# Second mixer of a two-block transformer kernel: score products in split single-pass form, weight units between near steps, releases by tile, gates by tanh, two weight splits moved

## The reference

```python
x = x + rms_norm(hybrid_mixer(rms_norm(x, g1), ...), g2)
x = x + rms_norm(conv_ffn(rms_norm(x, g3), ...), g4)
```

```python
proj = hn @ w_in          # a_qk, a_v, a_o, a_gates, b_q, b_k, b_v, b_r, b_lr
# half A: mLSTM, 4 heads, both directions
qk  = silu(dwconv3(a_qk)); q_a, k_a = qk halves (k scaled by 1/8)
s   = (q k^T) * exp(d_intra - m);  h = (s v) / max(|s.sum|, exp(-m))
y_a = sigmoid(a_o) * head_rms_norm(h_fw + h_bw)
# half B: gated linear attention, 4 heads, both directions
o   = ((q k^T) with per-channel decay exp(b_t - b_s)) v
y_b = silu(b_r) * head_rms_norm(o_fw + o_bw)
return concat(y_a, y_b) @ w_out
```

## Time and profile before

| | us |
|---|---|
| three runs | 1351.3, 1355.44, 1361.3 (median 1355.44) |
| profiled execution | 1353.95 |
| its span (first to last instruction) | 1351.9 |
| PE busy in the span | 1303.8 (96%) |
| DVE, ACT, POOL busy | 684.3, 377.6, 770.8 |
| mean granted clock of PE | 0.978 |

### The profile page before, as it was taken

How to read it: one execution, slowest core, us unless ns; L and a number is a source line. 1 busy time by engine, 2 the same in 40 slices (tenths; PEclk the granted TensorE clock), 3 DMA queues, 4 the chain that set the end, 5 groups by cost and what they waited for, 6 DMA issues and landing times.

```text
span 1351.9 us, 16095 instructions
## 1 busy us (share of the span) xinstructions
PE 1303.8 (96%) x6428; PEld 1063.4 (79%) x6428; DVE 684.3 (51%) x905; ACT 377.6 (28%) x666; POOL 770.8 (57%) x472
## 2 busy tenths in 40 slices
PE   7999999999999999999999989988899999999996
PEld 5788888878888888888877868657788888888885
DVE  5453653777444431223867883585487644431002
ACT  4322354322121210103246452463232211111000
POOL 6754523576666656677765344130839866656662
PEclk9999979999999999999999989999899999999998
DMA  7212211232333223333222122100222333323331
GB/s 274 78 64 78 78 32 63 94 94 94 94 97 106 91 90 97 97 110 111 94 91 93 38 73 64 32 16 24 101 93 95 94 95 102 101 71 97 96 96 63
DMA packets 35418, 117.19 MB, mean 87 GB/s; under 512 B 3944, under 2 KB 4456, under 8 KB 35216
## 3 DMA queue, kind: packets, MB, share of 16 engines
q1 hardware_dynamic: 34272, 114.13, 26.5%
q10 hardware_dynamic: 1072, 2.03, 0.4%
HBM read 114.05 MB, written 2.10 MB: 86 GB/s over the span
## 4 chain that ended last, share of the span: by engine, by line
PE 86%; DVE 9%; ACT 3%; issue 1%; DMA 1%; POOL 0%; SPq 0%; POOLq 0%; DVEq 0%; ACTq 0%
PE PS L437 26%; PE PS L439 25%; PE PS L438 25%; DVE ACC L1549 2%; PE PS L630 1%; PE PS L876 1%; PE PS L607 1%; DVE LVS L1943 1%; PE PS L977 1%; PE PS L471 1%; PE PS L472 1%; PE PS L474 1%; DVE TMP L1927 1%; DMA RAW<-in_w 1%; DVE WT L2042 1%
## 5 line engine op out<-in xcount | busy, mean ns | idle before, releaser
L394 POOL TENSOR_TENSOR WL<-RAW,WH 128x1024 fp32r<-128x1024 f32 (+2 forms) x226 | 515.2, 2280 | 18.9
L391 POOL TENSOR_SCALAR WH<-RAW 128x1024 fp32r<-128x1024 f32 (+2 forms) x226 | 237.9, 1053 | 489.5 <-DMA RAW<-in_w 473.5
L437 PE MATMUL PS<-AH,WH 128*128 128x512 f32 x896 | 353.1, 394 | 8.2 <-DVE AL L1539 8.0
L438 PE MATMUL PS<-AL,WH 128*128 128x512 f32 x896 | 350.4, 391 | 0.0
L439 PE MATMUL PS<-AH,WL 128*128 128x512 f32 x896 | 350.3, 391 | 0.0
L437 PEld LDWEIGHTS PS<-AH,WH 128*128 128x128 f32 x896 | 169.3, 189 | 46.9 <-issue 10.4
L439 PEld LDWEIGHTS PS<-AH,WL 128*128 128x128 f32 x896 | 169.2, 189 | 35.9
L438 PEld LDWEIGHTS PS<-AL,WH 128*128 128x128 f32 x896 | 169.5, 189 | 34.8 <-issue 0.2
L439 PE MATMUL PS<-SH,WL 128*128 128x512 f32 x352 | 136.9, 389 | 0.0
L437 PE MATMUL PS<-SH,WH 128*128 128x512 f32 x352 | 136.9, 389 | 0.0
L438 PE MATMUL PS<-SL,WH 128*128 128x512 f32 x352 | 136.9, 389 | 0.0
(11 more groups left out here) (330 smaller groups left out, 1846.1 us busy)
## 6 DMA issues: line engine op xcount, KB each, us to landing
RAW<-in_w SPq DMA_DIRECT2D x163, 512.0 KB, 3.5
...
```

What stands on the lines that cost most here:

```text
L391: nc.gpsimd.tensor_scalar(WH[:, slot, 0:width], RAW[:, slot, 0:width], 1.0, 1.0, ALU.mult, ALU.mult).then_inc(s_hi, 1)
L394: nc.gpsimd.tensor_tensor(WL[:, slot, 0:width], RAW[:, slot, 0:width], WH[:, slot, 0:width].bitcast(F32), ALU.subtract).then_inc(s_split, 1)
L437: nc.tensor.matmul(o, lh, rh, start=start, stop=False)
L438: nc.tensor.matmul(o, lh, rl, start=False, stop=False)
```

## The change

1. Scores: keys and queries of half A are rounded by ACT (`score_high`, new tiles KQH) and their remainders taken by DVE (`score_low`, AKL, AQL); each float32 score product becomes three fp32r matmuls. The stabilisers' selector and rows are split likewise (SELR, MSTK with high rows 0 to 7 and low rows 32 to 39), so that one fp32r matmul of 40 rows replaces each float32 one.
2. Units: `level_steps(0)` now computes kq1 (into banks 4 and 5, where its keys stay for pair 1), and aq comes behind it (banks 0 and 1); `decay_gates(0)` moves ahead of the third b_v unit. br 3 moves from steps 4 to 6 to steps 7 to 9, and `turn_output` of half B one step later.
3. By tile: ACT copies a b_v tile as soon as PE has ended it (`s_vt`), and ao overwrites a bank as soon as that is copied; av likewise, in banks 0, 1, 6 and 7.
4. Gates: sigmoid(a_o) becomes tanh(a_o / 2) + 1, the missing factor 0.5 goes into `gated`. Silu of b_r is taken for m = 0 and 1 before the recurrence and as r * (1 + tanh(r / 2)) for m = 2 and 3 (`gate_product`), with 4 in the root's scale. The roots of the last head's step have their table loaded in step 16.
5. Splits: wo2+4 and wo2+5 are split behind the four YL.
6. Exponentials: ACT's off-diagonal ones no longer wait for DVE's exponents (`s_ad`), only for the buffer (`s_mo`). `state_sum(2)` moves from step 15 behind the loop, two of the head squares into pair 1's steps, gate_read(3) from step 7 to 10; the column of ones in VA is written by ACT.

```diff
-("ao", 4), ("aq", 2), ("kq1", 2), ("ak", 2), ("av", 4)
+("ao", 4), ("kq1", 2), ("aq", 2), ("ak", 2), ("av", 4)
-        CBANK = (4, 5, 7, 6)
+        CBANK, VBANK, KQ = (0, 1, 7, 6), (0, 1, 6, 7), (0, 4)
 # POOL
-            split_range(UNITS["wo2"][0] + 4, UNITS["wo2"][0] + NS)
             for m in range(H2):
                 pool.wait_ge(s_y2h, m + 1)
...
-            split_range(UNITS["wo2"][0] + NS, UNITS["ffn2"][0] + NS)
+            split_range(UNITS["wo2"][0] + 4, UNITS["ffn2"][0] + NS)
 # PE
-            value_unit("bvb", 0, 2)
             decay_gates(0)
+            value_unit("bvb", 0, 2)
             key_query_unit("q0", 0, 1)
-            value_unit("bvc", 0, 3)
-            pe.wait_ge(s_vb, NT)
+            value_unit("bvc", 0, 3, handed=s_vt)
             for n in range(4):
-                value_unit("ao", n, n)
+                value_unit("ao", n, n, free=s_vb if n == 0 else None)
...
-            level_steps(0, UNITS["aq"][0])
-            key_query_unit("kq1", 0, 0)
-            key_query_unit("kq1", 1, 1)
+            level_steps(0, UNITS["kq1"][0])
+            pe.wait_ge(s_msk, NT)
+            key_query_unit("aq", 0, CBANK[0])
+            key_query_unit("aq", 1, CBANK[1])
...
-                    ins = nc.tensor.matmul(pb[d], SEL[0:8, r * P:(r + 1) * P], MROWS[d], start=True, stop=True)
+                    ins = nc.tensor.matmul(pb[d], SELR[r, q:q + P], MSTK[r, :], start=True, stop=True)
...
-                nc.tensor.matmul(pb[2 + n % 2], AK[hp:hp + HD, ht, tokens(j)], AQ[hp:hp + HD, ht, :],
-                                 start=True, stop=True).then_inc(s_ms2, 1)
+                nc.tensor.matmul(pb[2 + n % 2], kh[:, tokens(j)], qh, start=True, stop=False)
+                nc.tensor.matmul(pb[2 + n % 2], kl[:, tokens(j)], qh, start=False, stop=False)
+                nc.tensor.matmul(pb[2 + n % 2], kh[:, tokens(j)], ql, start=False, stop=True).then_inc(s_ms2, 1)
...
-                if 4 <= n < 7:
-                    output_gate(n - 1)
+                if 7 <= n < 10:
+                    output_gate(n - 4)
 # ACT
-                A(AO[:, t, :], pb[4 + t], ACT.Sigmoid, scale=RC[:, t:t + 1]).then_inc(s_aof, 1)
+                A(AO[:, t, :], pb[4 + t], ACT.Tanh, scale=RCH[:, t:t + 1]).then_inc(s_aof, 1)
...
             stabilisers_copied(0)
+            for m in range(2):
+                act.wait_ge(s_brr, m + 1)
+                A(BR[:, m, :], BR[:, m, :], ACT.Silu).then_inc(s_br, 1)
+            A(COL[:, 247:248], EPS_C, ACT.Exp)
             heads_out(1)
+            act.wait_ge(s_gs, 2 * NT)
+            score_high(1)
...
+                    if n >= 3:
+                        act.wait_ge(s_mo, n - 2)
                     for d in range(2):
                         c = CG[:, j, d, h + H2 * d:h + H2 * d + 1]
-                        act.wait_ge(s_ad, 2 * n + d + 1)
...
+                    for d in range(2):
+                        act.wait_ge(s_ad, 2 * n + d + 1)
                         A(WT[:, n % 3, d, tokens(j)], WT[:, n % 3, d, tokens(j)], ACT.Exp).then_inc(s_w, 1)
 # DVE
-            scaled, tapped = {1: (2,), 3: (3,)}, {0: (1,), 4: (2,), 6: (3,)}
+            scaled, tapped = {0: (2,), 2: (3,)}, {1: (1,), 5: (2,), 7: (3,)}
...
-                    if n % NT == 3 and n > NT:
+                    if n in (7, 11):
...
+            state_sum(H2 - 2)
             state_out(H2 - 1)
             state_sum(H2 - 1)
```

More of the change, by code:

```diff
@@ L477, in side_by_side, with row_unit @@
                                     ins.then_inc(s_used, 1)
-            def row_unit(u, n, hi, lo, banks=4, each=None, rows=range(NT)):
+            def row_unit(u, n, hi, lo, banks=(4, 5, 6, 7), each=None, rows=range(NT), handed=None, free=None):
                 s = u % NS
@@ L484, in row_unit @@
                 for t in rows:
+                    if free is not None:
+                        pe.wait_ge(free, t + 1)
                     for kk in range(2):
@@ L487, in row_unit @@
                         c = slice(kk * T, (kk + 1) * T)
-                        ins = mm3(pb[banks + t], hi[:, k, tokens(t)], lo[:, k, tokens(t)], WH[:, s, c], WL[:, s, c],
+                        ins = mm3(pb[banks[t]], hi[:, k, tokens(t)], lo[:, k, tokens(t)], WH[:, s, c], WL[:, s, c],
                                   k == 0, k == DK - 1)
+                    if handed is not None and t < NT - 1:
+                        ins.then_inc(handed, 1)
                 return ins
@@ L808, in decay_gates, with value_unit @@
                                      start=True, stop=True).then_inc(s_gpr, 1)
-            def value_unit(name, n, k, each=None):
+            def value_unit(name, n, k, each=None, handed=None, free=None):
                 u = UNITS[name][0] + n
                 ready(u)
-                row_unit(u, k, GH, GL, each=each).then_inc(s_used, 1)
+                row_unit(u, k, GH, GL, each=each, handed=handed, free=free).then_inc(s_used, 1)
             ge(pe, s_sd["ple"], 1)
@@ L1489, in _ @@
                         stabilisers_copied(h + 1)
+                if n == NT * H2:
+                    A(COL[:, 247:248], EPS_C, ACT.Sqrt)
                 if n and n % NT == 0:
@@ L1499, in _ @@
                     scaled_states(n // NT - 1)
+                if n in (5, 11):
+                    m = 2 if n == 5 else 3
+                    act.wait_ge(s_brr, m + 1)
+                    A(TANH[m - 2][:], BR[:, m, :], ACT.Tanh, scale=0.5).then_inc(s_br, 1)
                 if n == 7:
                     act.wait_ge(s_ybq, 1)
[L1502 to L1507 removed]
+                    A(BSS[:, 0:8], BSS[:, 0:8], ACT.Sqrt, bias=EPS_C, scale=1.0 / DV)
+                    A(BSS[:, 8:16], BSS[:, 8:16], ACT.Sqrt, bias=prm("eps", 4), scale=4.0 / DV).then_inc(s_gn, 1)
+                if 13 <= n < 17:
+                    high_gated(range(n - 13, n - 12))
             scaled_states(H2 - 1)
@@ L2000, in _ @@
             conv_tapped(0)
+            conv_scaled(1)
             for l in range(NL):
@@ L2021, in head_squares @@
                                         mybir.AxisListType.X, ALU.add)
+            ge(dve, s_msh, 5)
+            V_.tensor_tensor(MSTK[32:40, :], MROWS[0], MSTK[0:8, :].bitcast(F32), ALU.subtract).then_inc(s_msl.sem, 1)
+            V_.tensor_tensor(MSTK[96:104, :], SQ[64:72, 1, :], MSTK[64:72, :].bitcast(F32), ALU.subtract
+                             ).then_inc(s_msl.sem, 1)
+            for n in range(NT, 2 * NT):
+                near_summed(n)
+                if n == NT + 1:
+                    score_low(0)
+                if n >= NT + 2:
+                    link(head_squares(YB, n - NT - 2, BSS, ACC[:]))
+            dve.wait_ge(s_gb, 2 * NT)
+            for m in range(2):
+                gate_read(m)
             def gated(h):
@@ L2110, in _ @@
                         ins.then_inc(s_ybq, 1)
+                if n == 3:
+                    score_low(1)
+                if n in (6, 12):
+                    gate_product(2 if n == 6 else 3)
                 if n == 8:
@@ L2168, in _masks @@
     masks[:, 6] = 2.0 * (s == t)
-    sel = np.zeros((P, 8, P), np.float32)
-    for i in range(8):
-        sel[i, i] = -1.0
+    sel = np.zeros((2, 40, H2, P), np.float32)
+    for h in range(H2):
+        sel[0, h, h] = sel[0, 32 + h, h] = -1.0
+        sel[1, H2 + h, h] = sel[1, 32 + H2 + h, h] = -1.0
     neg = np.zeros((P, 2, P), np.float32)
```

148 lines of the change are left out of this document (95 added, 53 removed).

## The result

| | before | changed |
|---|---|---|
| median of four runs each | 1356.84 us | 1337.86 us (1335.65 to 1340.55) |
| profiled execution, its span | 1353.95, 1351.9 | 1340.55, 1338.5 |
| mean granted clock | 0.978 | 0.983 |

The ratio is 0.9858 (0.9827 to 0.9889): 19.0 us faster, where 1337 was forecast.

The account below looks back on a forecast made before the run. Three PE waits and dear float32 products, all inside 714 to 921 us, were taken as what could be had. Terms -2.8 - 7.2 - 15.0 + 7.5 = -17.5 on 1353.95 gave 1336.5, from the median 1337.9; forecast 1337, range 1325 to 1351.

Parts of the forecast that it names:

- Up to pair 0's steps: Stretch before pair 0's steps: they start at 737.3 instead of 740.1, -2.8 us, bounds -1 and -4.4.
- ACT is not what PE waits for in the first step: Pair 0's first step: sparing ACT's 1.28 us table load before the a_o gates was given no gain there.
- Up to pair 1's steps: Pair 0's to pair 1's steps: convolution wait 2.0 us instead of 5.78, slow products gone; -5.6 of the part's -7.2.
- a gap of 2.0 is shorter than both that were followed by 1.2 GHz, so I take them as gone: Behind the convolution wait, before pair 1's steps: no products at 1.2 GHz any more, -1.8 us.
- The recurrence: Recurrence, 69.6 us before: -8.3 in its first window and -6.7 in its second, -15.0 us; bounds -8 and -21.
- 16 scores at three times 0.23 instead of 1.05 give -5.8: Recurrence, PE's work: each float32 score replaced by three products of 0.23 us, -5.8 us in all.
- hand-offs: Recurrence: 1.4 us added in the first window; in the second, 30.9 us taken above PE's floor of 27.
- PE's floor: Recurrence: PE's own work of 47.5 us; if that is all, the part reaches its bound of -21 us.
- hand-offs keep the recurrence slow: Rival, chance 0.22: cheaper scores gain nothing where PE waits for `weighted`; recurrence -8, total 1343.5 us.
- the half clock: Rival, chance 0.06: gaps between steps hold PE at 1.2 GHz through the recurrence, +40 us, total 1377.
- The end: Last mix to half A's turns: POOL's splits delay DVE; PE stalls 6 us, plus 1.5 at 1.2 GHz, +7.5.
- the end is free: Rival, chance 0.25: POOL's instructions miss DVE's, or half A's sum precedes them; end costs +0.5, total 1329.5 us.

Follow-up runs that it names:

- e1_late: Changed kernel, but POOL starts the splits of wo2+4 and wo2+5 only when DVE has done all four `gated`; 1331.2 us, ratio 0.9801.
- e4_ad: Changed kernel with ACT's off-diagonal exponentials waiting for DVE's exponents again; 1339.99 us, ratio 0.9863.
- e6_conv: Changed kernel with `conv_scaled(2)` moved from behind level 0 to behind level 1 of pair 1; 1335.36 us, ratio 0.984.
- e7_sum: e1_late with `state_sum(2)` back in step 15, ahead of the last two multiplications; 1334.92 us, ratio 0.9832.
- e5_before_late: Kernel before, with only its splits of wo2+4 and wo2+5 held until half A is gated; 1355.56 us, ratio 0.998.
- e8_gates: Changed kernel with Sigmoid for a_o and Silu for br 2 and 3 in place of tanh, without gate products; 1342.24 us, ratio 0.9887.
- e2_mid: Changed kernel with the splits of wo2+4 and wo2+5 back between YB and YL; 1334.23 us, ratio 0.9829.
- e3_fp32: Changed kernel with scores and stabilisers as single float32 products again, without rounding copies and remainders; 1340.02 us, ratio 0.9862.
- e10_ad_late: e1_late with ACT's off-diagonal exponentials waiting for DVE's exponents again; 1333.13 us, ratio 0.9832.

## Why the prediction was right, and where its terms were off

**Up to pair 0's steps (-2.8, in the profile +0.8).** The wait on the copy of b_v went as forecast, and PE waits for the chain of levels instead, 1.68 us. The two profiles differ in something ahead of the mixer: the changed kernel waited 1.79 us for L1613 at 688 where before waited 0.41 for the same instruction, and PEclk is 0.87 against 1.00 in 690 to 714, which is 3.1 us of PE's time. DVE and POOL show the wait of the changed kernel:

```profile
685.35 2.84 DVE L1613 TENSOR_TENSOR ACC<-ACC,SQ 128x512 f32<-128x512 f32 x1
```

```profile
684.97 2.67 POOL L405 TENSOR_TENSOR WL<-RAW,WH 128x1024 fp32r<-128x1024 f32 x1
```

It is the effect of the end again: L1613 took 0.68 us at 683.30, and 2.84 when it came 0.38 behind the start of a split's L405. The ten profiles of the changed code fall in two groups, whatever the edit. In five (the changed kernel, e1_late, e4_ad, e6_conv, e7_sum) L1613 came behind that L405, PE waited 1.79 to 1.81 us, and products behind it ran at 1.2 GHz; from PE's product there to pair 0's steps they have 51.0 to 52.7 us. In the other five L1613 came 1.1 us ahead of the L405 and took 1.53, PE waited 0.17 or less, and they have 49.6 to 49.8, all at full clock, where before had 52.1. By these the term is -2.3 to -2.5, with 0.3 to 0.5 too much forecast. Nothing in the change touches that place. What sets DVE and POOL in one order or the other is not shown; the two profiles of the kernel before (before, e5_before_late) have the short wait. One step of this part was wrong: "ACT is not what PE waits for in the first step". With the table load back, in e8_gates, PE waits 1.40 us there for ACT's SAB, so the tanh of a_o is worth 1.3 us.

**Up to pair 1's steps (-5.6, measured -3.8, in e1_late -5.4).** The wait was worked out as 2.0 us and is 2.50, and its end, counted from the start of the steps, came within 0.1 us of the working: DVE's `conv_scaled(2)` waits for the first ak unit, as e6_conv shows by moving it. What failed is the step "a gap of 2.0 is shorter than both that were followed by 1.2 GHz, so I take them as gone". After the same gap of 2.50 or 2.49 the products ran at 1.2 GHz in the profiles of the changed kernel, e2_mid, e3_fp32, e8_gates and e10_ad_late, and at full clock in e1_late, e4_ad and e7_sum. It is worth 1.5 us (77.9 against 76.4), and a forecast can only give it a chance.

**Pair 1's steps (-1.6, measured -1.8).** One stabiliser pair and 0.3 of idle time; right.

**The recurrence (-15.0, measured -16.6).** The whole was right and its inner terms were not, by amounts that cancelled. PE's busy time fell from 60.84 to 50.46 us, its idle time from 8.6 to 2.4. The first of these, 10.4, splits into 16 scores at 0.15 (2.4), three stabiliser pairs (4.6: each took 1.91, and now two take 0.43 and the one behind a score 0.24) and products at full clock instead of 1.2 GHz (0.05 of 69.4, 3.5); together 10.5.
- Failed: "16 scores at three times 0.23 instead of 1.05 give -5.8". The 0.23 was read from products of 128 rows behind each other; the first score pass, of 64 rows behind a product of 128, takes 0.43. The term is -2.4.
- Right in size, and not for the reason given: the stabilisers, -1.48 for a pair behind a product of 128 rows (-1.67 behind a score) against the 1.45 worked out. By e3_fp32 0.85 of it come with rows in two places of the array and 0.63 with the single pass.
- Left out: the 1.2 GHz in the recurrence of before, 3.5 us, which went with its long waits. The sum took PE's second window with 3.4 less, but gave most of it back as "hand-offs".
- PE's floor was put at 47.5 and is 50.5, most of it by the scores (and the bound from 47.5 alone is -22, not the -21 of the prediction: 69.6 less 47.5); the allowance for hand-offs of 7 us was too large, 2.4 are there, 1.29 of them in the wait for YB (forecast 1.5).
- The edits taken back one at a time cost 6.6 (`state_sum(2)`, 3.8 of it idle time), 4.0 (splits), 3.3 (scores and stabilisers), 1.5 (gates) and 0.7 beside the clock (exponentials). Each was measured with the others in place; with the clock in some of them they are not terms that have to add up to 16.6.

The rival "hand-offs keep the recurrence slow" (a part of -8) falls: PE is busy 50.46 of 52.90 us, and DVE, with 42.9 us of work, keeps up once its longest waits are away. The price of 40 us for the half clock falls too: PEclk is 1.00 throughout. But a weaker form lives in e2_mid, e4_ad, e7_sum and e10_ad_late, where 1.4 to 2.9 us of the recurrence were lost to 1.2 GHz behind waits of 0.94 to 3.76 us.

**The end (+7.5, measured +7.9).** A wait of 5.47 us (forecast 6) and 2.5 in the turns (forecast 1.5). The mechanism was tested by taking away only what makes DVE wait: with the splits later, e1_late has the four sums at 1.14 us and the end 6.8 us shorter. The rival "the end is free" falls with that. What e1_late still pays over before at the end, 1.1 us of wait, is `state_sum(2)` in front (0.8 us, put at 0.5) and POOL's last YL on the denominators (1.1), less the 0.8 that DVE had in hand.

By the Trainium skill, SBUF - State Buffer, "Who interferes with whom", a DVE instruction with two SBUF inputs blocks fully against a GpSimd one that reads SBUF; the trace agrees, 4.71 us against 1.14 for the same four, and adds that it holds for instructions of four columns (1.04 against 0.24 for two). That issue order could favour DVE is not seen in the changed kernel's end: POOL's L405 took 2.40 and 2.34 us there, no longer than the 2.40 it took in e1_late away from the sums. It is seen elsewhere: in e1_late an L1614 that started at 926.87 took its free 0.69 us, and POOL's L402, at 926.89, took 1.58 instead of 1.05.

**The sum.** -17.5 was forecast and 13.4 measured between the two profiled executions, 19.0 between the medians. Against the profiles the forecast is 4.1 too low; 3.1 us of slow products at 690 and 1.5 behind the convolution, which some of the other profiles don't have, are more than that. The time of 1337 was met by the median with the errors above partly against each other: that it came so near is partly luck.
